# Exchanging the feed-forward block's quadrant turns through HBM, on ScalarE's queue

## What is computed

```python
h2 = rms_norm(x, norm_ffn_g[l])
u = jnp.square(jax.nn.relu(jnp.einsum('bsd,df->bsf', h2, w_up[l])))     # 2048 -> 8192
x = x + jnp.einsum('bsf,fd->bsd', u, w_down[l])                         # 8192 -> 2048
return rms_norm(x, norm_final_g)
```

## Time and profile before

| | |
|---|---|
| median of 3 runs | 1476.49 us (1476.45 to 1476.63) |
| the profiled execution | 1476.18 us |
| its span, first to last instruction | 1474.4 us |
| PE busy | 1465.7 us |
| DVE busy | 1190.9 us |
| ACT busy | 766.8 us |
| read from HBM, written | 296.45 MB, 2.10 MB |

### The profile page before, as it was taken

One profiled execution on the slowest core, in us unless ns is written; L12 is line 12 of the kernel. 1 busy time (PEld: TensorE's weight loads), 2 busy tenths in 40 slices (PEclk: granted clock), 3 DMA queues, 4 the chain that ended last, 5 costly groups with the idle time before them and its releaser, 6 DMA issues.

```text
span 1474.4 us, 18772 instructions
## 1 busy us (share of the span) xinstructions
PE 1465.7 (99%) x6968; PEld 1279.8 (87%) x6968; DVE 1190.9 (81%) x1558; ACT 766.8 (52%) x986; POOL 15.0 (1%) x21
## 2 busy tenths in 40 slices
PE   9999999999999999999999999999999999999997
PEld 8888888888888888888888888888888888888886
DVE  7977887776577788777799988888897888889877
ACT  7656565444455555444445555555554555555553
POOL 0000000000000000000000000000000000000000
PEclk9999999999999999999999999999999999999999
DMA  9556544667655566556765665656666656655563
GB/s 333 191 169 211 184 154 164 229 203 241 213 180 184 186 199 206 194 200 200 248 233 181 202 219 201 218 185 207 217 204 202 208 199 226 214 199 193 198 209 114
DMA packets 149801, 299.33 MB, mean 203 GB/s; under 512 B 5232, under 2 KB 5360, under 8 KB 149488
## 3 DMA queue, kind: packets, MB, share of 16 engines
q1 hardware_dynamic: 149168, 297.51, 59.9%
q10 hardware_dynamic: 576, 1.06, 0.2%
HBM read 296.45 MB, written 2.10 MB: 202 GB/s over the span
## 4 chain that ended last, share of the span: by engine, by line
PE 98%; issue 1%; DVE 1%; POOLq 0%; POOL 0%; DVEq 0%; ACT 0%
PE acc L545 88%; PE acc L827 3%; PE banks L776 3%; PE acc L776 1%; PE banks L564 1%; PE banks L583 1%; PE banks L573 0%; PE banks L591 0%; DVE ta_lo L1775 0%; PE banks L680 0%; PE banks L696 0%; PE banks L695 0%; PE banks L693 0%; PE acc L603 0%; DVE final L1787 0%
## 5 line engine op out<-in xcount | busy, mean ns | idle before, releaser
L865 ACT ACTIVATE whi<-raw 128x1024 fp32r<-128x1024 f32 x542 | 569.2, 1056 | 577.3 <-PE acc L545 517.9
L1222 DVE TENSOR_TENSOR wlo<-raw,whi 128x1024 fp32r<-128x1024 f32 x542 | 655.1, 1223 | 213.1 <-ACT whi L865 208.5
L545 PE MATMUL acc<-whi,ta_hi 128*128 128x512 f32 x1308 | 497.4, 380 | 0.0
L545 PE MATMUL acc<-wlo,ta_hi 128*128 128x512 f32 x1308 | 495.7, 379 | 0.0
L545 PE MATMUL acc<-whi,ta_lo 128*128 128x512 f32 x1308 | 495.7, 379 | 0.0
L545 PEld LDWEIGHTS acc<-whi,ta_hi 128*128 128x128 f32 x1308 | 247.2, 189 | 36.7 <-issue 1.2
L545 PEld LDWEIGHTS acc<-whi,ta_lo 128*128 128x128 f32 x1308 | 247.2, 189 | 35.1
L545 PEld LDWEIGHTS acc<-wlo,ta_hi 128*128 128x128 f32 x1308 | 247.3, 189 | 34.5
L545 PE MATMUL acc<-whi,tb_hi 128*128 128x512 f32 x560 | 212.3, 379 | 0.0
L545 PE MATMUL acc<-wlo,tb_hi 128*128 128x512 f32 x560 | 212.2, 379 | 0.0
L545 PE MATMUL acc<-whi,tb_lo 128*128 128x512 f32 x560 | 212.2, 379 | 0.0
(11 more groups left out here) (208 smaller groups left out, 1049.2 us busy)
## 6 DMA issues: line engine op xcount, KB each, us to landing
raw<-in_w_in SPq DMA_DIRECT2D x64, 1024.0 KB, 5.2
raw<-in_w_up SPq DMA_DIRECT2D x64, 1024.0 KB, 5.3
raw<-in_w_down SPq DMA_DIRECT2D x57, 1024.0 KB, 5.0
raw<-in_w_gate SPq DMA_DIRECT2D x32, 1024.0 KB, 5.3
raw<-in_w_att SPq DMA_DIRECT2D x16, 1024.0 KB, 5.0
raw<-in_w_ret SPq DMA_DIRECT2D x16, 1024.0 KB, 5.0
raw<-in_w_out SPq DMA_DIRECT2D x16, 1024.0 KB, 5.0
raw<-in_w_down SPq DMA_DIRECT2D x14, 512.0 KB, 4.3
```

The lines of the kernel that those rows point to most:

```text
L545: last = nc.tensor.matmul(paired(acc[B.parity][:, t, :]), a[:, k, tok], halves_in_turn(b), start=(k == 0 and n == 0), stop=(k == (B.ends + ...
L865: nc.scalar.activation(whi[:, B.ring_at(u), :], raw[:, B.raw_at(u), :], ACT.Copy).then_inc(hi_ready, 1)
L1222: V_.tensor_tensor(wlo[:, at, :], raw[:, B.raw_at(u), :], whi[:, at, :].bitcast(f32), ALU.subtract).then_inc(lo_ready, 1)
```

## The change

1. DVE turns a block with four transposes of 128 x 256 (`turn_in_quads`), which turn 32 x 32 squares where they stand, into `buf[3]`. The squares then lie in the wrong group of 32 rows.
2. ACT stores the result to a buffer in HBM (`park`, one DMA of 512 KB), waits for it, and loads it back to `buf[1]` with four DMAs (`fetch`), one per group of 32 rows, which puts the squares in place. The five DMAs are issued by ACT, between its splits.
3. The halves of `tb` are made from `buf[1]` in the new layout (`hi_from_exchanged`, `lo_from_exchanged`), one block later than before: the first block's during the third, the third's during D0, the fourth's during D1. The mixtures too are formed in D1.
4. In the last quarter PE does D0 and D1 up to their sixth unit, then the last two units of D0, then those of D1, since the fourth block's operands come later.
5. The second weight sum has a buffer of its own (`sum_two`) in place of `buf[1]`. The final norm's gains `gfin` are loaded behind the last weights, not ahead of the output projection.

The rest of the diff gives the blocks of a quarter and the groups of seven products a table of their own, set to the same groups as before (2 with 3 at the boundary, 0 with 1 late).

```diff
+BOUNDARY = (2, 3, 3)
+LATE = {0:(0,1,3)}
...
+            self.down = [Block(D0, 8, q), Block(D1, 8, q, -UCH)]
+            self.down_end = [Block(D0, 8, q, 6), Block(D1, 8, q)]
...
+        sum_two = place("sum_two", [P, UCH, COLS], f32, at_f + 8 * K)
...
+        parking = nc.dram_tensor("parking", (GROUPS, P, TILES * COLS), f32, kind="Internal").ap()
+        in_quads = buf[3][:].rearrange("p t (o n) -> p (t o) n", n=S)
+        exchanged_at = buf[1][:].rearrange("p t (i n) -> p (t i) n", n=S).rearrange("p i (a n) -> p i a n", n=SQ)
+        by_block = exchanged_at.rearrange("p i a n -> p a i n")
+        by_tile = exchanged_at.rearrange("p i (m t) n -> p m t i n", t=TILES)
...
-            sp.wait_ge(ret_full, 4)
-            sp.dma_start(gfin[:], g_fin.partition_broadcast(P)).then_inc(fin_full, 16)
...
+                pairs = [n // 2 for n in Q.units]
+                if last:
+                    for j in range(2):
+                        load_rows(Q.down[j], w_down, j * COLS, q * D, range(3))
+                    for j in range(2):
+                        load_rows(Q.down_end[j], w_down, j * COLS, q * D, range(3, 4))
+                else:
+                    for j in range(2):
+                        load_rows(Q.down[j], w_down, j * COLS, q * D, range(pairs[j]))
+                load_rows(Q.J, w_down, 2 * COLS, q * D, range(pairs[2]))
+                if Q.boundary:
+                    load_left(Q.boundary, q * D)
+                    load_right(Q.boundary, q * D)
+                load_rows(Q.K, w_down, 3 * COLS, q * D, range(pairs[3]))
+                if last:
+                    if AGAIN:
+                        sp.wait_ge(folded, q * FOLDS_OF_QUARTER)
+                    sp.dma_start(gfin[:], g_fin.partition_broadcast(P)).then_inc(fin_full, 16)
...
+                pe.wait_ge(t_free, q * 4 + (T_STAGE6 + 2))
+                gemm(Q.down[0], tb_hi, tb_lo, 0, 4)
+                if last:
+                    pe.wait_ge(t_free, q * 4 + (T_STAGE6 + 3))
+                    gemm(Q.down[0], tb_hi, tb_lo, 4, 6)
+                    gemm(Q.down[1], tb_hi, tb_lo, 0, 6)
+                    pe.wait_ge(t_free, q * 4 + (T_STAGE6 + 4))
+                    for j in range(2):
+                        gemm(Q.down_end[j], tb_hi, tb_lo, 6, 8)
+                else:
+                    if Q.units[0] > 4:
...
-                gemm(B[5], tb_hi, tb_lo, 0, B[5].ends + 1)
-                gemm(B[6], tb_hi, tb_lo, 0, UNITS - 2)
...
+                    split(E, 0, 2)
+                    if i > 1:
+                        hi_from_exchanged(Q.turn(q, i - 1), i - 2)
+                    split(E, 2, 4)
...
+                        split(E, 4, 5)
+                        if i:
+                            park(q * 4 + i, i - 1)
+                        split(E, 5, 7)
+                    if i:
+                        fetch_next(Q, q, i, first)
+                    split(tail, 7, 8)
...
+                    split(Q.down[1], 1, 4)
+                    hi_from_exchanged(Q.turn(q, 4), 3)
+                    split(Q.down[1], 4, 5)
+                    mixed_hi_of(GROUPS - 1, q * MIXES_OF_QUARTER)
+                    split(Q.down[1], 5, 6)
+                    if last:
+                        for j in range(2):
+                            split(Q.down_end[j], 6, 8)
...
+                    residual_squares(Q.down_end[0], 0, down_sq, buf[1])
...
+            def park(n, g):
+                act.wait_ge(quads_turned, n)
+                act.dma_start(parking[g], in_quads.rearrange("p o n -> p (o n)")).then_inc(parked, 16)
+            def fetch(g, n):
+                for o in range(QUADS):
+                    act.dma_start(exchanged_at[o * SQ:(o + 1) * SQ].rearrange("f i a n -> f i (a n)"),
+                                  parking[g].rearrange("(i f) (o n) -> o f i n", f=SQ, o=QUADS)[o]).then_inc(exchanged, 16)
+            def fetch_next(Q, q, i, first):
+                act.wait_ge(parked, (q * 4 + i) * 16)
+                if i > 1:
+                    act.wait_ge(t_free, q * 4 + (T_STAGE6 + i - 1))
+                elif AGAIN and not first:
+                    act.wait_ge(mixed_set, q * MIXES_OF_QUARTER * MIXED)
+                elif not first:
+                    act.wait_ge(mixed_set, q * MIXED)
+                fetch(i - 1, Q.turn(q, i))
...
+            def hi_from_exchanged(n, g):
+                act.wait_ge(exchanged, n * QUADS * 16)
+                for h in range(2):
+                    to = tb_hi[:, g * GCH + h * UCH:g * GCH + (h + 1) * UCH, :].rearrange("p m (t i n) -> p (m t) i n", t=TILES, n=SQ)
+                    nc.scalar.activation(to, by_block[:, h * GCH:(h + 1) * GCH], ACT.Copy).then_inc(t_hi, 1)
...
-                    turn_among(B[i], q * 4 + (T_STAGE6 + i - 1), buf[0][:], u_ready, q * 4 + i, ((4, 0, 10), (5, 10, 14)))
...
-                split(B[5], 0 if last else 2, 3)
-                add_residual(B[4], 0)
-                split(B[5], 3, 4)
-                mixed_tokens(q)
-                split(B[5], 4, 6)
-                dve.wait_ge(mixed_hi_ready, q + 1)
-                V_.tensor_tensor(mixed_lo[:], mixed, mixed_hi[:].bitcast(f32), ALU.subtract).then_inc(mixed_lo_ready, 1)
...
+                mixed_tokens(Q.turn(q, 4), q * MIXES_OF_QUARTER)
+                lo_from_exchanged(q * 4 + 16, 3)
...
+                    split(Q.down_end[0], 6, 8)
+                    split(Q.down_end[1], 6, 7)
+                    add_residual(Q.down_end[0], 0)
+                    split(Q.down_end[1], 7, 8)
...
+                split(Q.J, done, ready)
+                add_residual(Q.down_end[1], 1)
...
+            def turn_in_quads(n):
+                dve.wait_ge(u_ready, n)
+                if later(n - 1):
+                    dve.wait_ge(parked, (n - 1) * 16)
+                for o in range(QUADS):
+                    piece = V_.transpose(in_quads[:, o, :].rearrange("p (m t n) -> p m t n", t=TILES, n=SQ),
+                                         by_chunk(buf[0][:])[:, :, :, o * SQ:(o + 1) * SQ])
+                piece.then_inc(quads_turned, 1)
...
+            def lo_from_exchanged(n, g):
+                for h in range(2):
+                    dve.wait_ge(t_hi, n * 2 + (h - 1))
+                    hi, lo = [a[:, g * GCH + h * UCH:g * GCH + (h + 1) * UCH, :].rearrange("p m (t i n) -> p (m t) i n", t=TILES, n=SQ)
+                              for a in (tb_hi, tb_lo)]
+                    V_.tensor_tensor(lo, by_block[:, h * GCH:(h + 1) * GCH], hi.bitcast(f32),
+                                     ALU.subtract).then_inc((first_half, t_free)[h], 1)
...
+            def sums_for_seven(G, mixes):
+                E, u = G.entries, G.at
+                left_up, left_low, right_low, right_up = corners(G)
+                T1, T2, T3 = weight_sums(G)
+                dve.wait_ge(raw_full[E.slot(u)], E.filled(u))
+                dve.wait_ge(corner_full, G.n * 16 + 16)
+                V_.tensor_tensor(T1, left_up, right_up, ALU.add).then_inc(sum_set, 1)
+                dve.wait_ge(raw_full[E.slot(u + 2)], E.filled(u + 2))
+                dve.wait_ge(sum_set, G.sums(1))
+                V_.tensor_tensor(T2, T1, right_low, ALU.add).then_inc(sum_set, 1)
+                split(E, u - 2, u - 1)
+                dve.wait_ge(mixed_lo_ready, mixes)
+                V_.tensor_tensor(T3, right_up, right_low, ALU.add).then_inc(sum_set, 1)
                 sums_lo(G, 0)
...
+            def mixed_tokens(turn, before):
+                dve.wait_ge(exchanged, turn * QUADS * 16)
+                (a11, a21), (a12, a22) = [[by_tile[:, half, t] for t in range(TILES)] for half in (slice(0, UCH), slice(UCH, GCH))]
+                m = [mixed[:, c].rearrange("p k (i n) -> p k i n", n=SQ) for c in range(MIXED)]
+                V_.tensor_tensor(m[0], a21, a22, ALU.subtract).then_inc(mixed_set, 1)
+                V_.tensor_tensor(m[1], a11, a21, ALU.subtract).then_inc(mixed_set, 1)
```

More of the change, by code:

```diff
@@ L761, in stage6 @@
-                gemm(B[5], tb_hi, tb_lo, 0, B[5].ends + 1)
-                gemm(B[6], tb_hi, tb_lo, 0, UNITS - 2)
-                if not last:
+                Q = Quarter(q, first, last)
+                for i in range(GROUPS):
+                    (E, tail), G = Q.up[i], Q.late[i]
+                    if first and i == 0:
+                        pe.wait_ge(h2T_ready, 3)
+                        gemm(E, ta_hi, ta_lo, 0, 6)
+                        pe.wait_ge(first_half, T_STAGE5 + 4)
+                        gemm(E, ta_hi, ta_lo, 6, 7)
+                        pe.wait_ge(h2T_ready, 4)
+                        gemm(E, ta_hi, ta_lo, 7, 8)
+                    else:
+                        gemm(E, ta_hi, ta_lo, 0, 6)
+                        if G:
+                            seven_products(G)
+                        gemm(tail, ta_hi, ta_lo, 6, 8)
@@ L832, in rest @@
             def rest(B):
-                for u in range(2, UNITS):
+                for u in range(B.ends + 1):
```

(44 more changed lines are left out.)

387 lines of the change are left out of this document (207 added, 180 removed).

## The result

| | before | after |
|---|---|---|
| median of 11 runs each | 1476.53 us | 1480.74 us (1479.90 to 1481.53) |
| the profiled execution | 1476.18 us | 1481.53 us |
| its span | 1474.4 us | 1479.7 us |
| PE, DVE, ACT busy | 1465.7, 1190.9, 766.8 us | 1466.2, 1103.8, 767.0 us |

The changed kernel takes 1.0028 times as long (95% interval 1.0019 to 1.0037): 4.2 us more. The forecast was 1479.2, with a range of its own from 1478.7 to 1480.0 inside a stated one from 1476.4 to 1481.5; the time lies in the stated range alone, beyond the 0.2% that I counted as no change. The profiled execution is the slowest of the eleven, 5.35 us above that of before.

What follows compares the result with a forecast made beforehand. PE's full queue of matmuls was taken to bound the kernel. Last-quarter waits of 1.6 + 1.1 = 2.7 us, the exchange hidden, gave 1478.9 on the profiled 1476.18, 1479.2 on the median; own range 1478.7 to 1480.0, stated 1476.4 to 1481.5.

Steps and rivals of the forecast that it cites:

- What bounds the kernel: Whole kernel: PE's full queue of matmuls, busy 1465.7 of 1474.4 us; unchanged matmul number can gain almost nothing, 0.4 us.
- DVE's 84 us: In the 16 turns DVE loses 84 us of busy time, worth nothing since PE does not wait for it.
- the transposes: Each turn: 16 transposes of 32x256 become four of 128x256, taken at 436 ns each, 1.8 us a turn.
- (c): In the turns: transposes go by rows, 1.74 us each, PE waits 1.5 us in 16 turns; 1503 us; chance 0.03.
- (e): Whole kernel: DVE's 84 us come through, or the end's 0.4 us goes; 1476.1 at best; chance 0.02.
- The exchange: Each turn: store 4.2 us and loads 5 us, sum 9.2, hidden by the lead; issuing five DMAs takes ACT 2 us.
- rival (a): In 16 turns: round trip not hidden, store plus loads beyond 13 us, PE waits; at 15 us, 1511; chance 0.10.
- Rival (d): Exchange's loads: scattered short runs take 24 us each, PE waits 18 us in 16 turns; about 1767; chance 0.02.
- steps 1 to 3: Last quarter (E: J's first matmul): D0's residual from E-4.98, squares to E-2.51, J's units 0 and 1 split by E+0.94.
- Step 4: Last quarter: second corner load issued at E+1.38, landing 4.8 us later (4.6 to 5.3); first weight sum 3.6 us later.
- Steps 5 to 8: Last quarter: PE loses 1.6 us in J and 1.1 at the third product's fold; from there folds and end as before.
- the first step of rival (a): In the turns: the beginning of the unhidden round trip's times, taken into the stated range, which ends at 1481.5.

Runs made afterwards that it cites:

- the old turning: Changed kernel without the exchange: 16 transposes of 32x256 turn each block straight into the exchanged layout, store and four loads gone; 1480.28 us, ratio 1.0039.
- the loads issued late: Kernel with D0's residual behind D1's last and J's first splits (1476.64), loads of each quarter's first three turns issued directly ahead of their copies; 1484.18 us.
- the run with two more entries: Kernel with D0's residual later, late-group table given two added entries (D0 and D1, J and K corners of the third block), DVE's list reordered; 1493.76 us, ratio 1.0116.

## Why the prediction was right, and where it was short

- **What bounds the kernel, DVE's 84 us, the transposes.** Right. PE stayed at 163.00 of 163 us; DVE's 87 us came through nowhere, and giving them back (the old turning) lost nothing. A transpose of 128x256 took 413 ns; I had taken 436 between bounds of 436 and 1740. Rivals (c) and (e) are out.
- **The exchange.** Right in its terms: store 3.9 us (4.2 taken), loads 5.0 (5 taken), no wait of PE in 16 turns. The 13 us of rival (a), 14.2 with the issuing, is near what the loads issued late showed: 13.8 cost nothing, 15.4 cost 0.7 us, and a turn that starts from full lead hid 16.5. ACT's five issues took 2.1 us (0.35 and 1.76; 2 taken). Rival (d) is out: with 1 KB contiguous on both sides the loads took 5.0 us, not 24. The Trainium skill, VectorE: DVE Perf Modes, The three transpose paths, warns of a plain copy that transposes by strides when the innermost destination stride is large. By the measured loads its condition was not met here.
- **Last quarter, steps 1 to 3.** Right. Residual at E-5.10 (E-4.98 said), squares done at E-2.51 (E-2.51), second corner issued at E+1.26 (E+1.38).
- **Step 4.** This is the term that was short: "the second lands 4.8 us later (4.6 to 5.3)". It took 6.48 here, and the first sum came at E+7.84 in place of E+6.18. Fifteen of the sixteen parts landed in 4.14 to 4.76 us, as I had said; the load was late by its last part alone, with a 16 KB instruction packet under way, which the sum had no term for. I had followed the stall of D0's residual to J's splits and to the corners, but not to D1's unit 7 as well, which stands behind the same addition: it frees the place of J's third pair, whose 1 MB then went out only 3.6 us ahead of the corners. With that pair at its old time the load took 5.0 us, the gaps 3.1, and the median fell by 0.7. The pair's nearness alone does not do it: at 3.7 to 3.9 us behind a pair the same load landed after 4.6 to 4.9 us where no such packet came.
- **Steps 5 to 8.** Right in kind. The sum being 1.66 us later than I said, 2.7 becomes 4.4, and 0.11 at D1's unit 7 makes 4.5: the 4.52 that PE's timeline shows. The wait in J split into two, at unit 4 and unit 5, since unit 4 became late too; the third product lost 1.15 (1.1 said).
- **The chances.** I gave the forecast 0.50 below the 0.2% bound and 0.26 above. It came out above, by the mechanism of the forecast and none of the rivals. That it still lies in the stated range is luck: my sum ended at 1480.0, and I had gone on to 1481.5 for the first step of rival (a), which did not come.
- **Left open.** The medians differ by 4.2 us and the gaps of the traced execution, the slowest of eleven, by 4.5; no run moves the instruction fetch, so its share in the late landing is argued from the traces, not shown by an experiment.

## What to carry to other kernels

When an instruction is delayed in an engine's list, follow everything behind it in that list to the transfers that it releases, and not just the one on the path: here a load that nobody waited for was pushed near the one that mattered, and moving it back won 0.7 us of 4.2. A load is as late as its last part, so look at what else the DMA engines carry meanwhile, instruction fetches too, before the load ahead is blamed. Time freed on an engine that nobody waits for buys nothing by itself; new work that is to use it is decided by where its operations stand in that engine's list, not by the mean idle time. A round trip through HBM behind a lead of some three units can be free, and its limit can be measured by issuing its second half late.

## What the runs showed of the hardware that was not expected

How long the second corner load (512 KB) took to land, by how far ahead of it the nearest 1 MB load of the same queue had been issued, and whether an instruction packet of 16 KB was fetched meanwhile, in the traces of this case but that of the run with two more entries, which has more such packets:

| 1 MB load ahead by | instruction packet | landed after | loads |
|---|---|---|---|
| 3.7 to 3.9 us | none | 4.6 to 4.9 us | 8 |
| 2.7 to 2.9 us | none | 5.6 to 6.0 us | 6 |
| 5.6 us or more | within 0.6 us of the issue | 5.0 to 5.9 us | 9 |
| 5.6 us | 4.1 to 4.4 us behind the issue | 4.7 to 4.8 us | 5 |
| 4.0 us | 0.5 to 1.1 us behind the issue | 5.4, 6.5, 6.5 us | 3 |
| 2.7 us | 4.0 us behind the issue | 7.2 us | 1 |

In the last two rows one of the sixteen parts came 0.7 to 1.8 us behind the other fifteen. Holding back the load behind it changed nothing. The Trainium skill, DMA: Bandwidth & Descriptors, Queues, rings and completion order, says that on each DMA engine the descriptors of one queue are consumed in ring order; the second row agrees with it, and no trace here tells of one DMA engine alone.

In the run with two more entries in the table PE stood 2.4 us and then 1.4 us for nothing that the profile shows, some 20 us behind three waits of 0.8 to 1.4 us, and from 1119 to 1125, behind the first of these stands, the granted clock read 0.50 (the 1.2 GHz level), with matmuls 0.427 us apart in place of 0.216. In the changed kernel it stayed at 1.00 through the waits of 1.3, 1.9 and 1.1 us. The slower matmuls added about 2.6 us to that run.

```profile
1119.00:1125.00 6.00, 5.01 (x13) 3.81 (x12) 2.45 (x2) 0.41 (x1) 0.00 (x0) 0.50 0.57 184
```

The row is a window of that run, columns as in the first fence of the result.
